# All projections: the products with the weights' high part first, those with the low part last

## The reference, cut to what matters

```
x += 0.5 * SwiGLU_1(rms(x))
x += mixer_i(rms(x))             # layer 0: mLSTM, layer 1: gated DeltaNet with a convolution
x += CrossAttn(rms(x), memory K/V)   # 4 heads over 256 memory tokens
x += 0.5 * SwiGLU_2(rms(x))
rms_norm(x, g) = x * rsqrt(mean(x * x) + EPS) * g
```

## Time and profile before

| | |
|---|---|
| median of 3 runs (lowest to highest) | 2787.82 us (2783.12 to 2792.76) |
| the profiled execution's own time | 2787.62 us |
| its span | 2786.1 us |
| TensorE busy | 2698.9 us (97%), 21474 matmuls |
| weight loads busy | 2590.0 us (93%) |
| DVE, ACT, GpSimd busy | 1302.1, 896.5, 196.8 us |
| mean granted TensorE clock | 0.982 |

### The profile page before, as it was taken

The page is one execution under the profiler, slowest core; times in us unless marked ns, Lnnn a source line. Parts: engine busy times, 40 slices in busy tenths (PEclk is TensorE's granted clock), DMA queues, the critical chain, the costliest instruction groups (busy, mean ns, idle before and its releaser), DMA issues.

```text
span 2786.1 us, 49878 instructions
## 1 busy us (share of the span) xinstructions
PE 2698.9 (97%) x21474; PEld 2590.0 (93%) x21474; DVE 1302.1 (47%) x2086; ACT 896.5 (32%) x1129; POOL 196.8 (7%) x171
## 2 busy tenths in 40 slices
PE   7999999998989999999999999999799989999998
PEld 7999999887876999999999999999697977999998
DVE  5444334235484444432444434768435673444422
ACT  4333222234233333322222222543334332333322
POOL 2000000011010100000000000001220100100000
PEclk9999999999999999999999999999899999999999
DMA  4333324222383233332233332223214482333331
GB/s 124 90 90 102 94 81 117 54 76 70 122 286 131 84 91 90 96 102 82 84 91 95 106 94 72 66 66 90 55 43 136 156 281 93 92 90 90 104 94 52
DMA packets 476866, 280.69 MB, mean 101 GB/s; under 512 B 24939, under 2 KB 465004, under 8 KB 476706
## 3 DMA queue, kind: packets, MB, share of 16 engines
q1 hardware_dynamic: 449720, 230.83, 29.3%
q0 software_dynamic: 8704, 33.56, 3.3%
q10 hardware_dynamic: 18314, 14.45, 1.6%
HBM read 261.31 MB, written 17.69 MB: 100 GB/s over the span
## 4 chain that ended last, share of the span: by engine, by line
PE 86%; DVE 6%; ACT 3%; issue 3%; DMA 1%; POOL 1%; SPq 0%; ACTq 0%; DVEq 0%; POOLq 0%
PE ACC L436 24%; PE ACC L437 24%; PE ACC L438 24%; PE ACC L1133 2%; PE M L2205 1%; DVE w_lo L531 1%; ACT w_hi L525 1%; DMA raw<-in_xa_w_k 1%; PE ACC L2205 1%; DVE cache L1234 1%; PE M L1487 1%; PE M L2367 1%; DVE w_lo L546 1%; PE M L1562 1%; PE M L1516 1%
## 5 line engine op out<-in xcount | busy, mean ns | idle before, releaser
L436 PE MATMUL ACC<-xg_hi,w_hi 128*128 128x260 f32 x3968 | 1128.7, 284 | 11.3 <-DVE w_lo L907 7.6
L437 PE MATMUL ACC<-xg_lo,w_hi 128*128 128x260 f32 x3968 | 1123.1, 283 | 0.0
L438 PE MATMUL ACC<-xg_hi,w_lo 128*128 128x260 f32 x3968 | 1122.5, 283 | 0.0
L531 DVE TENSOR_TENSOR w_lo<-raw,w_hi 128x1024 fp32r<-128x1024 f32 (+1 forms) x326 | 421.8, 1294 | 976.0 <-ACT w_hi L525 975.7
L436 PEld LDWEIGHTS ACC<-xg_hi,w_hi 128*128 128x128 f32 x3968 | 749.9, 189 | 12.9 <-issue 8.5
L438 PEld LDWEIGHTS ACC<-xg_hi,w_lo 128*128 128x128 f32 x3968 | 750.4, 189 | 0.0
L437 PEld LDWEIGHTS ACC<-xg_lo,w_hi 128*128 128x128 f32 x3968 | 750.4, 189 | 0.0
L525 ACT ACTIVATE w_hi<-raw 128x1024 fp32r<-128x1024 f32 (+1 forms) x326 | 363.5, 1115 | 1145.5 <-PE ACC L438 1129.0
L437 PE MATMUL ACC<-hid_lo,w_hi 128*128 128x260 f32 x1408 | 399.3, 284 | 0.0
L436 PE MATMUL ACC<-hid_hi,w_hi 128*128 128x260 f32 x1408 | 398.2, 283 | 0.0
L438 PE MATMUL ACC<-hid_hi,w_lo 128*128 128x260 f32 x1408 | 398.0, 283 | 0.0
(11 more groups left out here) (556 smaller groups left out, 3269.2 us busy)
## 6 DMA issues: line engine op xcount, KB each, us to landing
raw<-in_ffn_w_gate SPq DMA_DIRECT2D x88, 512.0 KB, 3.8
raw<-in_ffn_w_up SPq DMA_DIRECT2D x88, 512.0 KB, 3.8
raw<-in_ffn_w_down SPq DMA_DIRECT2D x64, 704.0 KB, 4.6
cache<-in_cache_mem_k POOLq DMA_DIRECT2D x16, 1024.0 KB, 7.8
cache<-in_cache_mem_v POOLq DMA_DIRECT2D x16, 1024.0 KB, 8.1
raw<-in_gd_w_in SPq DMA_DIRECT2D x32, 512.0 KB, 4.2
raw<-in_ml_w_in SPq DMA_DIRECT2D x24, 512.0 KB, 4.0
raw<-in_xa_w_q SPq DMA_DIRECT2D x16, 512.0 KB, 4.4
```

Of the source, the lines that this page charges most:

```text
L436: pe.matmul(out, wh, hi[:, k0 + k, m], start=begin, stop=False)
L437: pe.matmul(out, wh, lo[:, k0 + k, m], start=False, stop=False)
L438: mm = pe.matmul(out, wl, hi[:, k0 + k, m], start=False, stop=end)
L531: dve.tensor_tensor(w_lo[:, j % 2, 0:n], raw[:, (j + d) % 4, 0:n], w_hi[:, j % 2, 0:n].bitcast(F32), ALU.subtract).then_inc(w_split, 1)
```

## The change

`pe_unit` waits for `w_hi_done` at its start instead of `w_split`. It first takes lines 436 and 437 for all pieces and sides, in the order of before; then it waits for `w_split`; then it takes line 438 for all pieces, side 1 first. Hooks are called by a count of matmuls where `apart` is set and there are two sides (k = 2 after 12 matmuls, k = 5 after 30, as before); in all other units a hook for k is still called before piece k of the first part. `second` moves from `extra` to `turned`, called before side 1 of the first part. No other engine's program changes, and the number of matmuls stays.

```diff
--- before.py
+++ after.py
@@ -404,7 +404,7 @@
                 return memg_hi, memg_lo
             return xg_hi, xg_lo
 
-        def pe_unit(pe, ph, j, i, extra=None, apart=True):
+        def pe_unit(pe, ph, j, i, extra=None, apart=True, turned=None):
 
             t = j // 2 if ph.per_tile == 2 else j
             pair, slot = t % 2, j % 2
@@ -413,7 +413,7 @@
             hi, lo = rhs_of(ph)
             k0 = (j % 2) * FH if ph.per_tile == 2 else 0
             first, last = (j % 2 == 0, j % 2 == 1) if ph.per_tile == 2 else (True, True)
-            pe.wait_ge(w_split, i * 4 + (u + 1))
+            pe.wait_ge(w_hi_done, i * 4 + (u + 1))
             if first and not (tau < 2 and isinstance(i, int) and i == 0):
 
                 pe.wait_ge(acc_free, i * (4 // ph.per_tile) + (tau - 1))
@@ -422,20 +422,33 @@
                 order = [(k, [h]) for h in sides for k in range(ph.kn)]
             else:
                 order = [(k, sides) for k in range(ph.kn)]
-            for n, (k, these) in enumerate(order):
+            def place(h):
+                if ph.kind == "memkv":
+                    return ACC[:, 2 * pair, 0:NMEM], slice(0, NMEM)
+                return ACC[:, 2 * pair + h, 0:TH], slice(h * TH, h * TH + TH)
+            turn = [(k, h) for k, these in order for h in these]
+            low_turn = [(k, h) for h in reversed(sides) for k in range(ph.kn)]
+            whole = apart and len(sides) == 2
+            told = 0
+            for n, (k, h) in enumerate(turn):
+                due = ph.kn * 2 * n // (3 * len(turn)) if whole else k
+                while extra and told <= due:
+                    extra(told)
+                    told += 1
+                if turned and n == ph.kn:
+                    turned()
+                out, m = place(h)
                 wh = w_hi[:, slot, k * P:(k + 1) * P]
-                wl = w_lo[:, slot, k * P:(k + 1) * P]
-                begin, end = first and k == 0, last and k == ph.kn - 1
-                if extra and n * ph.kn % len(order) == 0:
-                    extra(n * ph.kn // len(order))
-                for h in these:
-                    if ph.kind == "memkv":
-                        out, m = ACC[:, 2 * pair, 0:NMEM], slice(0, NMEM)
-                    else:
-                        out, m = ACC[:, 2 * pair + h, 0:TH], slice(h * TH, h * TH + TH)
-                    pe.matmul(out, wh, hi[:, k0 + k, m], start=begin, stop=False)
-                    pe.matmul(out, wh, lo[:, k0 + k, m], start=False, stop=False)
-                    mm = pe.matmul(out, wl, hi[:, k0 + k, m], start=False, stop=end)
+                pe.matmul(out, wh, hi[:, k0 + k, m], start=first and k == 0, stop=False)
+                pe.matmul(out, wh, lo[:, k0 + k, m], start=False, stop=False)
+            pe.wait_ge(w_split, i * 4 + (u + 1))
+            for n, (k, h) in enumerate(low_turn):
+                due = ph.kn * (2 * len(turn) + n) // (3 * len(turn))
+                while extra and told <= due:
+                    extra(told)
+                    told += 1
+                out, m = place(h)
+                mm = pe.matmul(out, w_lo[:, slot, k * P:(k + 1) * P], hi[:, k0 + k, m], start=False, stop=last and k == ph.kn - 1)
             mm.then_inc(mm_done, 1)
 
         def pe_norm_tok(pe, r):
@@ -468,13 +481,12 @@
                         pe.wait_ge(hid_ready, FC * ph.ff + FC - (1 if k == 0 else 0))
                     if k == 2 and j in low:
                         low[j]()
-                    if 2 * k == ph.kn and j == 0 and second:
-                        second()
                     if k == 5 and j in mid:
                         mid[j]()
                 if j in before:
                     before[j]()
-                pe_unit(pe, ph, j, 0, extra, not (j == 0 and (r is not None or 0 in mid and not second) or j < 2 and ph.kind == "down"))
+                pe_unit(pe, ph, j, 0, extra, not (j == 0 and (r is not None or 0 in mid and not second) or j < 2 and ph.kind == "down"),
+                        second if j == 0 else None)
                 if j == 0 and r is not None:
                     pe_norm_tok(pe, r)
             if before or mid:
```

## The result

The changed kernel takes 2818.76 us (median of 4 runs, 2812.52 to 2820.77). The kernel before took 2789.22 us in the same session, and the ratio is 1.0106 (95% interval 1.0084 to 1.0127): about 29.5 us slower. The forecast was 2806.5, range 2796 to 2815. The sign is right, the size is too small, and the median lies 3.8 us above the range.

A forecast was written before the change was run, and what follows sets the result against it. TensorE was taken to bound the kernel almost throughout. Costs of 9.4 (norm units), 2.5 (start), 3.3 (hooked first units) and 3.5 (`xk`, `xv`) sum to 18.7 us, giving 2806.5 us against the median; range 2796 to 2815.

The forecast's parts named there:

- start: Program's first unit: 20 matmuls follow piece 7 instead of 6; 2.5 us lost, between 1.7 (full clock) and 3.7 (half clock).
- seven norm units: First units after a norm: piece 7 of the low activations wanted earlier, 1.46 us each, 0.65 in `xq_0`; 9.4 us lost.
- xk and xv: Memory keys and values: hooks wanted after 10 matmuls instead of 15; 1.7 us per layer, 3.5 in all, bounds 0 to 4.8.
- hooked first units: Unit 0 with `apart` off: hook wanted after 20 matmuls instead of 30; `gd_q`, `gd_z` 1.2 us each; 3.3 in all.
- whole units: Reordering the projection matmuls itself: same count, pace kept at 0.12 us a matmul, so 0 us.
- The later wait for `w_lo`: Unit starts: they still wait for the read-out behind `w_lo` in DVE's program; 0 won, at most 13.1 us.
- Rival A: Unit starts: the wait for `w_lo` is what holds them, so 13.1 us come back, giving 2793.4 us; chance 0.06.
- Rival B: Norm phases: unit 1 waits anyway, partly hiding the new stalls; 9.4 us shrink to 4.6 or less, 2801 to 2797; chance 0.10.
- rival C: Seven new norm stalls: clock falls, 20 matmuls at half clock each, 2 us each, 14 in all, 2820 us; chance 0.06.
- The pace: Projection matmuls: no step shorter than another at 0.12 us, new order keeps it; 0, one nanosecond each being 18.4 us.
- rival D: Low part alone runs at another pace; 18.4 us per ns a matmul either way; chance 0.05 for gain, 0.03 for loss.

The follow-up runs named there:

- g1: The changed kernel with the old matmul order and old wait back in the program's very first unit alone; 2813.7 us, ratio 1.0092 to the kernel before.
- e1: The changed kernel with the old order back in the first unit of the eight phases that begin with a norm; 2804.51 us, ratio 1.0057.
- e2: The changed kernel with the old order back in all 32 units of `xk` and `xv`; 2810.88 us, ratio 1.0083.
- e5: The kernel before with the new order and wait only in seven hooked first units (`ml_o`, `ml_out`, `gd_q`, `gd_v`, `gd_z`, two `xo`); 2794.43 us, ratio 1.0028.
- e3: New order only in two-sided `apart` units; old in norm, hooked first, first two `down` units, `xk`, `xv`; 2789.22 us, ratio 0.9999 to the kernel before.
- e4: The changed kernel, new order everywhere, but the wait for `w_split` back at each unit's start; 2815.27 us, ratio 1.0095 to the kernel before.
- f1: The kernel before, but DVE reads the accumulator out before making the next `w_lo`, except in gate/up and conv; 2775.0 us, ratio 0.9958.
- f2: The changed kernel, but DVE reads the accumulator out before the next `w_lo`, except in gate/up and conv; 2794.22 us, ratio 1.0027 to the kernel before.
- f3: New order only in units whose hooks kept their place, plus DVE reading the accumulator out before the next `w_lo`; 2780.0 us, ratio 0.9971 to the kernel before.
- f6: The kernel before, with DVE's read-out ahead of the next low part only in the ML and GDN projections (proj, projz); ratio 0.9976.
- f5: The kernel before, with DVE's read-out ahead of the next low part only in the q, `xk` and `xv` phases; ratio 0.9979.
- f4: The kernel before, with DVE's read-out ahead of the next low part only in the down and out phases; ratio 1.0005.

## Why the prediction was right in sign and too small in size

The runs price the parts one by one. In the last column stand the sums by ratio:

```
part                         predicted   profile after   runs
start (g1)                      2.5          3.6          3.9
seven norm units (e1 - g1)      9.4         10.2          9.8
xk and xv (e2)                  3.5          6.8          6.4
hooked first units (e5)         3.3          4.2          7.8
whole units (e3)                0            2.3         -0.3
sum                            18.7         27.1         27.6
```

The whole is 24.9 us in the profile (2 less than its parts: other stretches went the other way) and 29.5 in the runs; each part of the last column is a difference of ratios and uncertain by some 3 to 6 us.

- **The later wait for `w_lo` wins nothing.** Right, as far as e4 can tell. Rival A is out: the earlier trace rows named `w_lo`, but the read-out behind it in DVE's program ended the wait.
- **Norm units.** Right: by the start of unit 2, 1.55 to 1.60 us in six of them and 0.73 in `xq_0`, where 1.46 and 0.65 were forecast. `xg_lo` begins when it was said to. What the forecast left out is that the stream starts up again behind the stall: the first matmul there is followed after 0.22 us (416.79 to 417.01) and not 0.12. Rival B is out.
- **The start.** The mechanism was right and the size was a midpoint that no row supported: the half-clock end of the bounds, 3.7, was met (3.6), and g1 and e4 show that the thin stream holds the clock down.
- **Hooked first units: the term that failed most.** The waits came as forecast, `gd_q` 1.2, `gd_z` 1.2 to 1.5, `ml_o` 0.9, `ml_out` and `gd_v` 0.3, together 4.2. The rest up to 7.8 is not in the waits. A part of it is seen in e5's trace: the clock that falls behind the wait in `gd_q` takes 3.1 us more.
- **`xk` and `xv`.** In layer 1 the trace has 1.9 us, where the prediction had 1.7; that this is close is partly luck, for 1.0 of it is in `xk_1`, where the prediction had none, and 0.9 in `xv_1`, where it had all. In layer 0 it has 4.9 (2.3 and 2.5), and the difference is two stretches at the lower clock, which make unit 5 of `xk_0` 1.3 and unit 7 of `xv_0` 1.5 us longer than in layer 1. Windows after (before, all windows from 798 to 806 and the one from 838 to 843, where unit 7's hook ran, were at 1.00):

```profile
800.00:802.00 2.00, 1.54 (x11) 1.44 (x12) 1.78 (x3) 0.50 (x1) 0.00 (x0) 1.00 0.82 228
802.00:804.00 2.00, 2.00 (x9) 1.64 (x9) 2.00 (x12) 0.00 (x0) 0.00 (x0) 0.62 0.79 223
804.00:806.00 2.00, 2.00 (x12) 2.00 (x11) 0.82 (x6) 0.13 (x1) 0.71 (x1) 0.53 0.72 212
...
847.00:850.00 3.00, 3.00 (x14) 2.94 (x15) 0.00 (x0) 0.00 (x0) 0.00 (x0) 0.50 0.89 349
```

- **The clock had no term in the sum, and this is the step at fault.** Beside the start, where 2.5 us held a part for it, the prediction met it only as rival C, at the seven norm stalls, with a chance of 0.06 and 14 us, and put it at nothing in the hooked units and in `xk` and `xv` without a reason. In the profiled run it did not fall at the norm stalls, but at others. The size can be worked out from the granted clock that is on record for each execution, as (1 - clock) x span, in us, and the rest of the span:

```
kernel    executions   (1 - clock) x span   rest of the span
before        87             50.7               2736.4
changed        4             61.3               2754.9
g1             4             58.4               2753.8
e1             6             56.5               2746.7
e2             6             57.6               2752.4
e3            12             46.9               2739.8
e5            12             54.0               2740.0
f1            10             47.4               2726.4
f2            12             60.5               2732.5
f3            12             48.6               2728.6
```

These are means; the standard error is 0.4 us for the kernel before and 1 to 2.5 for the others in the first column, 0.2 to 1.2 in the second. It is an estimate: a slow stretch in which TensorE waits anyway costs less than its share, and then the second column is too low. The changed kernel is 18.5 us longer in the rest, where the prediction's sum was 18.7, and 10.6 us longer by the clock, of which the sum held 0.8 at the start. The size of the error is therefore the clock's. That the rest agrees so closely is partly luck, since e3's pace is 3.4 us in it where the sum had nothing, and the seven norm units (e1 less g1) are 7.1 where the sum had 9.4.

- **Where the clock was lost.** e5 has the new order in the seven hooked units alone, and its clock share is 3.3 us more than before, with an error of 1.4. f2 and f1 differ only in TensorE's order and wait, both without the long norm stalls, and f2 has 13.1 us more of it, with an error of 1.6; f3, with the new order in the whole units alone, has 1.2 more than f1, within the errors. So the slow clock comes with the new order in the first units (the start among them), `xk` and `xv`, and the seven norm stalls are not needed for it. Which stall makes it fall is seen in single places (`gd_q` in e5, `gd_z` in e4 and f2, two in layer 0's memory phases) and is argued for the others; in the changed kernel's unit 2 of `gd_k` (1748 to 1751) it falls with no wait of more than 0.3 us in the 7 us ahead of it.
- **The pace** was taken as 0, and the time as a whole moves by 0 (e3). The table shows that two things meet in this: the rest is 3.4 us longer, of which the steps above explain some 2, and the clock's share is 3.8 us shorter. Why it is shorter there was not tried. The two sides of rival D, 18 us each, were far too large.

The range ended at 2815 because it left out "most of C". Had the sum had a clock term of this size, the forecast would have been near 2816 and the range would have reached beyond 2820.

What stays open: how often a stall of 1 to 2 us makes the clock fall, and why it falls where no wait stands ahead of it.

## What to carry to other kernels

Grouping the high products first makes every stream input (activations, hook operands) wanted after two thirds of the matmuls that hid it before, so read each producer's slack from the timeline before reordering; here 0.27 us of slack turned into a stall of 1.3 in seven places. A wait that is named for one product of an engine may be held by the next instruction in that engine's program: moving the wait gave 0, and moving the read-out ahead of the split gave 11.7 us. Where TensorE's stream gets thinner or gets new stalls, give the clock a term of its own in the sum, and split measured times into the clock's share and the rest over all executions: one profile is one draw.

## What the runs showed of the hardware that was not expected

- The same stall (1.48 and 1.49 us, same hook) was followed by half clock in one execution and by full clock in another; the unit took 11.47 and 8.39 us.
- The step of a 128x260 matmul depends a little on the order: with the products grouped it is 120.0 ns in all four gate/up phases, and with the old order 119.3 in most and 120.3 in one or two. Which ones is not tied to the phase: it is the first in the profiles of before, f1 and f6, `ffn1_1_gu` in those of e5 and f5, and the first two in f4's. 841 against 836 matmuls in 100 us shows the difference.
- Most of the spread of one kernel from execution to execution goes with the granted clock: over 87 executions of the kernel before, the span has a standard deviation of 3.9 us, and without (1 - clock) x span 2.1 us.
